# Weights, tokens, keys and vectors handed over in the order of use, and results stored turned, in a GLA, Fourier and PEER inference step

## The chip, the cores and the metric

The kernel runs on one core of one Trainium2 chip. The metric is the device time of one execution in microseconds. The median of the runs of the kernel before is 5125.47 us (3 runs, 5105.1 to 5128.31).

## What is computed

One step of a two-layer network over 128 context tokens and 512 latent tokens of width 1024. Both token groups go through the same layers with the same weights. Cut to what matters (the Fourier part and the rotary embedding are left out):

```python
def _trunk(x, cond, rope_pos, init_state, ...):
    for l in range(DEPTH):                                    # 2 layers
        sh1, sc1, g1, sh2, sc2, g2 = _modulation(cond, w_mod[l], b_mod[l])
        h = _rmsnorm(x, norm1[l]) * (1 + sc1) + sh1
        mix, s_f, s_b = _token_mixer(h, ...)                  # w_in, gated linear attention, Fourier, gates, w_out
        x = x + g1 * mix
        h = _rmsnorm(x, norm2[l]) * (1 + sc2) + sh2
        x = x + g2 * _peer(h, w_query[l], sub_keys[l], expert_u[l], expert_v[l])
    return _rmsnorm(x, final_norm)

def _peer(h, w_query, sub_keys, expert_u, expert_v):
    qry = (x @ w_query).reshape(n, 8, 2, 128)                 # 8 heads, two halves
    s = jnp.einsum('nhpd,hpkd->nhpk', qry, sub_keys)          # 128 keys per half
    ...                                                       # 16 best of each half, 16 best of their sums
    a = jax.nn.gelu(jnp.einsum('nd,nhkd->nhk', xb, expert_u[ib]))
    return jnp.einsum('nhk,nhkd->nd', wb * a, expert_v[ib])   # 128 rows of u and of v for each token
```

## The kernel before, in words

All data are float32. Tokens stand turned in the on-chip memory: `xT` and `hT` hold 128 of the 1024 features on the partitions, 8 chunks, and 640 token columns (128 of the context, then 512 latent). The program is written engine by engine, with semaphores; on each engine the steps of several programs are merged by `weave`, which sorts them by due times in a table, so the order on each engine is fixed when the kernel is built. It runs in stages: the context's mixer of layer 0 with the modulation (0 to 330 us of the trace); the latent mixer of layer 0 with the context's expert stage (to 1051 us); the latent expert stage of layer 0 with the context's mixer of layer 1 (to 2735 us); latent mixer and context experts of layer 1 (to 3488 us); latent experts of layer 1 (to 5053 us); the last norm.

**Weights.** SP (the queue of the sync engine) loads 0.25, 0.5 or 1 MB pieces into four slots of 8 KB a partition, in the order of the list `FILLS`. A piece is loaded as soon as the operand four places before it in the list has been used up (`released`). `cols_of` cuts a piece from the weight matrix in its own layout: 128 partitions, 8 chunks of rows, and runs of 128 or 256 columns, 512 or 1024 bytes. A piece is a `wraw`, `fraw` or `slot` buffer in the rows. In front of the list SP loads the constants and the tokens (`xin`, lines 543 to 546).

**Start.** GpSimd loads fifteen small vectors as rows. TensorE turns vectors and tokens by products with the identity (lines 1093 to 1103), VectorE copies them into `cols` and `xT`, ScalarE and VectorE make `scond`, the gate of the conditioning vectors. Then the modulation begins: 24 products of a layer with 1 MB of `w_mod` each, eight of them ahead of the first norm.

**Keys.** For each of the 8 heads of an expert stage GpSimd loads the two sets of 128 keys (`skey`, two buffers), TensorE turns them (`keys`, line 936), ScalarE copies them (`skT`), and `scores` multiplies the queries with them, one head later. GpSimd loads the key of head h when that of head h-2 has been turned. The expert gathers stand behind the keys in GpSimd's queue.

**Latent merge.** For each z of 8, TensorE makes four products of three terms each (gate of the attention, gate of the Fourier part, both outputs). Each of the four weight pieces is loaded, copied by ScalarE to a rounded high part (`whigh`, `fhigh`) and subtracted by VectorE to a low part (`wlow`, `flow`, line 1576); ScalarE makes the sigmoids and VectorE the gating (`sg`, `mT`) in between. The four pieces of the next z take the four slots as they are used up.

**Expert rows.** For each pick GpSimd gathers 128 rows of 4 KB of `expert_u` and, eight picks later, of `expert_v` (lines 629 and 636), for the latent tokens through rings of six and four buffers. VectorE makes the dot products (line 1731); for the latent tokens TensorE sums the v rows through diagonal matrices, for the context VectorE does (`acc`).

**End.** The last norm writes `hT` (lines 1443 and 1448); TensorE turns it back (line 1088), VectorE copies it to `y_nat` (line 1816), SP stores it in five pieces (lines 594 and 597).

Of the kernel before, what the change touches and what calls it, by code (L numbers as in the profile page):

```python
# [22 lines left out]
F32 = mybir.dt.float32  # L23
# [6 lines left out]
P = 128  # L30
D = 1024
KC = D // P
# [81 lines left out]
def fill_values():  # L114

    loads, values = SLOTS * [0], []
    for n, what in enumerate(FILLS):
        loads[n % SLOTS] += 2 if what[0] == "qk" else 1
        values.append(16 * loads[n % SLOTS])
    return values  # L120
# [106 lines left out]
def build(nc, x_prompt, x_sample, state_gla, c, c_ctx, w_mod, b_mod, norm1, w_in, w_af, b_af, w_ab, b_ab,  # L227
          gla_norm, w_gla_out, w_four_out, w_out, norm2, w_query, sub_keys, expert_u, expert_v, final_norm,
          consts, fourier, y_prompt, y_sample, new_state):
# [26 lines left out]
    cols0 = place("cols0", [P, 24])  # L256
    scond = place("scond", [P, KC, 2])
    cols = [place(f"cols{l}", [P, 80]) for l in range(DEPTH)]
# [72 lines left out]
    def peer_area(s, at, queries_at):  # L331
# [20 lines left out]
        a.skey = [place(f"skey{i}_{tag}", [P, 2, P], at=q) for i in range(2)]  # L352
# [21 lines left out]
    y_nat = [place("y_nat_ctx", [P, NT[CTX], D], at=[zone]), place("y_nat_lat", [P, NT[LAT], D], at=[area[CTX].end])]  # L374
    s_at = [area[LAT].end]
    xin = place("xin", [P, T // P, D], at=s_at)
    rows0 = place("rows0", [24, P], at=s_at)
    rows = [place(f"rows{l}", [80, P], at=s_at) for l in range(DEPTH)]

# [8 lines left out]
    with ExitStack() as ctx:  # L388
# [22 lines left out]
        def sem(name):  # L411
# [3 lines left out]
        s_const, s_tab, s_x, s_rows = sem("const_loaded"), sem("tables_loaded"), sem("x_loaded"), sem("rows_loaded")  # L415
# [7 lines left out]
        s_set, s_xt, s_xc = sem("constants_set"), sem("x_turned"), sem("x_copied")  # L423
        s_rowsT, s_cols = sem("rows_turned"), sem("cols_ready")
# [26 lines left out]
        s_qm, s_qc, s_kt, s_ktc, s_sm, s_sc = (sem("query_mm"), sem("query_copied"), sem("keys_turned"),  # L451
                                              sem("keys_copied"), sem("score_mm"), sem("scores_copied"))
# [8 lines left out]
        s_yt, s_yc = sem("y_turned"), [sem(f"y_copied_of{s}") for s in range(2)]  # L461
# [76 lines left out]
        def cols_of(w, l, c0, width):  # L538
            return w[l][:, c0:c0 + width].rearrange("(c p) n -> p c n", p=P)
# [1331 lines left out]
```

## Time and profile before

| what | value |
|---|---|
| runs, median (lowest to highest) | 5125.47 us (5105.1 to 5128.31) |
| profiled execution, its own time | 5096.34 us |
| its span, first to last instruction | 5094.5 us |
| busy: TensorE, VectorE, ScalarE, GpSimd | 79%, 58%, 26%, 56% of the span |
| moved | 1583.47 MB, 311 GB/s mean |
| of it gathers (queue q0) | 1346.63 MB in 370656 packets, 69.5% of 16 engines |
| of it SP's loads (queue q1) | 229.86 MB in 323856 packets, 14.4% of 16 engines |
| mean granted TensorE clock | 0.952 |

How to read it: a busy share is a mean over stages with different limits; what a stage waits for is read in that stage. In the rows PE is TensorE, PEld its weight loads, DVE VectorE, ACT ScalarE, POOL GpSimd, SPq the queue of SP. A row of the timeline has its start, its length, the engine, the line, what is written and read, how many instructions are merged in it, and in brackets how long the engine stood idle before it and what ended that. A row of DMA issues has the tile, the issuing queue, the count, the size of one and the median time from issue to landing.

### The profile page before, as it was taken

How to read it: one execution, taken by the hardware profiler on the slowest of the kernel's cores; microseconds unless marked ns; L12 is line 12 of the kernel's file. 1: busy time of each engine (PE TensorE's matmuls, PEld its weight loads, DVE VectorE, ACT ScalarE, POOL GpSimd, SP SyncE). 2: the span in 40 equal slices, each digit the busy share in tenths (PEclk: the TensorE clock that was granted, in tenths of full speed). 3: DMA queues.
4: the chain of work that ended last, by engine and by line, in shares of the span. 5: the costliest groups of instructions: out<-in, count | busy, mean ns of one | idle time of the engine just before them, and what ended most of it. 6: DMA issues, size and time to landing. Idle time of an engine off the chain costs nothing. (4 is left out here: it accounts for less than half of the span.)

```text
span 5094.5 us, 43662 instructions
## 1 busy us (share of the span) xinstructions
PE 4028.3 (79%) x13059; PEld 2047.3 (40%) x13059; DVE 2945.2 (58%) x6592; ACT 1314.6 (26%) x2679; POOL 2843.7 (56%) x2611
## 2 busy tenths in 40 slices
PE   7889678898788888788777977889877777776776
PEld 4675346653333333244324543565322222222222
DVE  1127997716555565565543699772556555655644
ACT  2433234511122232233111332451211111111111
POOL 0001665305767776777773066540477777777774
PEclk9999789899999999999999988899999999999999
DMA  6663988737999999999996298882599999999997
GB/s 227 199 186 126 327 321 286 241 95 277 381 397 376 400 396 371 366 400 406 407 390 226 84 337 305 304 268 86 200 366 367 370 393 381 375 382 365 369 392 288
DMA packets 699356, 1583.47 MB, mean 311 GB/s; under 512 B 52344, under 2 KB 368752, under 8 KB 698736
## 3 DMA queue, kind: packets, MB, share of 16 engines
q0 software_dynamic: 370656, 1346.63, 69.5%
q1 hardware_dynamic: 323856, 229.86, 14.4%
q10 hardware_dynamic: 4608, 4.20, 0.2%
q8 instruction: 104, 1.70, 0.1%
q14 instruction: 132, 1.08, 0.1%
HBM read 1575.78 MB, written 4.72 MB: 310 GB/s over the span
## 5 line engine op out<-in xcount | busy, mean ns | idle before, releaser
L657 PE MATMUL pair<-vbuf_lat,diag 128*128 128x512 f32 x4096 | 2024.7, 623 | 705.0 <-DMA vbuf_lat<-in_expert_v,idx_lat 679.3
L657 PEld LDWEIGHTS pair<-vbuf_lat,diag 128*128 128x128 f32 x4096 | 716.1, 192 | 1952.2 <-DMA vbuf_lat<-in_expert_v,idx_lat 1092.8
L636 POOL DMA_INDIRECT vbuf_lat<-in_expert_v,idx_lat x1024 | 1160.2, 1133 | 404.0 <-issue 203.8
L1731 DVE CUSTOM_DVE_ANT_0 ubuf_lat<-hT,ubuf_lat 128x1024 f32<-128x1024 f32 x768 | 935.2, 1224 | 722.9 <-DMA ubuf_lat<-in_expert_u,idx_lat 720.5
L629 POOL DMA_INDIRECT ubuf_lat<-in_expert_u,idx_lat x1024 | 1071.4, 1046 | 418.5 <-issue 234.4
L629 POOL DMA_INDIRECT ubuf_ctx<-in_expert_u,idx_ctx x256 | 289.1, 1129 | 564.7 <-DVE araw L1731 289.9
L1120 ACT ACTIVATE diag<-cst,coef 128x128 f32<-128x128 f32 x1024 | 326.8, 389 | 1064.5 <-DVE coef L1737 1060.6
L657 PE MATMUL pair<-hT,slot 128*128 128x512 f32 (+1 forms) x2048 | 580.7, 444 | 15.0 <-DVE hT L1450 14.9
L1731 DVE CUSTOM_DVE_ANT_0 ubuf_lat<-xnat,ubuf_lat 128x1024 f32<-128x1024 f32 x256 | 311.7, 1224 | 257.8 <-DMA ubuf_lat<-in_expert_u,idx_lat 256.8
L657 PEld LDWEIGHTS pair<-hT,slot 128*128 128x128 f32 x2048 | 322.5, 199 | 257.4 <-issue 254.6
L1120 ACT ACT_TABLE_LOAD x313 | 401.6, 1283 | 77.6 <-DVE mT_lat L1617 50.4
L636 POOL DMA_INDIRECT vbuf_ctx<-in_expert_v,idx_ctx x256 | 291.8, 1140 | 128.2 <-issue 77.7
L1777 DVE SCALAR_TENSOR_TENSOR acc<-vbuf_ctx,coef,acc 128x1024 f32<-128x1024 f32 x254 | 326.3, 1285 | 23.6 <-issue 0.9
L1120 ACT ACTIVATE gel<-araw 128x4 f32<-128x4 f32 x320 | 65.3, 204 | 1029.3 <-DVE araw L1731 1028.7
L1731 DVE CUSTOM_DVE_ANT_0 ubuf_ctx<-hT,ubuf_ctx 128x1024 f32<-128x1024 f32 x256 | 311.7, 1220 | 9.8 <-DMA ubuf_ctx<-in_expert_u,idx_ctx 4.2
L616 POOL DMA_DIRECT2D skey_ctx<-in_sub_keys x16 | 11.5, 720 | 382.3 <-PE pair L936 349.7
L616 POOL DMA_DIRECT2D skey_lat<-in_sub_keys x16 | 11.6, 723 | 314.2 <-PE pair L936 175.5
L657 PE MATMUL pair<-slot,scond 128*2 128x256 f32 x768 | 174.6, 381 | 2.0 <-DVE scond L1837 1.7
L657 PE MATMUL pair<-hmH,whigh 128*128 128x512 f32 x256 | 114.5, 447 | 56.8 <-DVE wlow L1576 45.3
L1649 DVE MAX8 top_lat<-sc_lat 128x8 f32<-128x128 f32 x256 | 55.3, 280 | 166.7 <-ACT sc_lat L1120 163.9
L657 PE MATMUL pair<-slot,hT 128*128 128x256 f32 x640 | 142.2, 381 | 0.0
L657 PE MATMUL pair<-hT,wraw 128*128 128x128 f32 (+1 forms) x768 | 134.6, 330 | 2.4 <-DMA wraw<-in_w_in 1.3
(319 smaller groups left out, 4024.8 us busy)
## 6 DMA issues: line engine op xcount, KB each, us to landing
slot<-in_w_mod SPq DMA_DIRECT2D x48, 1024.0 KB, 7.7
wraw<-in_w_in SPq DMA_DIRECT2D x80, 512.0 KB, 5.2
slot<-in_w_in SPq DMA_DIRECT2D x32, 1024.0 KB, 7.0
slot<-in_w_query SPq DMA_DIRECT2D x32, 1024.0 KB, 5.3
slot<-in_w_in SPq DMA_DIRECT2D x32, 512.0 KB, 4.9
wraw<-in_w_gla_out SPq DMA_DIRECT2D x32, 512.0 KB, 8.6
wraw<-in_w_out SPq DMA_DIRECT2D x32, 512.0 KB, 5.0
ubuf_lat<-in_expert_u,idx_lat POOLq DMA_INDIRECT x1024, 6.5
```

The source lines that it names most:

```text
L616: pool.dma_start(peer[s].skey[h % 2][:, :, :], sub_keys[l, h].rearrange("s k d -> k s d")).then_inc(s_skey[h % 2], 16)
L629: pool.indirect_dma_start(peer[s].u[n % ring_u][:, :], None, u_rows, bass.IndirectOffsetOnAxis(ap=index[:, p // PICKS, p % PICKS:p % PICKS ...
L636: pool.indirect_dma_start(peer[s].v[n % ring_v][:, :], None, v_rows, bass.IndirectOffsetOnAxis(ap=index[:, p // PICKS, p % PICKS:p % PICKS ...
L657: return pe.matmul(out, lhsT, rhs, start=first, stop=last)
L1120: return nc.scalar.activation(out, in_, fn, **kw)
L1649: v.max(a.top[:, h, q, r8], sc[:, h, q, :])
L1731: v.tensor_tensor_reduce(rows_of, x, rows_of, 1.0, 0.0, ALU.mult, ALU.add, araw[n % 3][:, p % GS:p % GS + 1]).then_inc(s_dot, 1)
L1777: last = stt(acc[:, :], row, coef[n % 3][:, j:j + 1], acc[:, :], ALU.mult, ALU.add)
```

## The change

The host hands every input over in the order in which the program takes it (`laid_out`): each weight piece as 128 partitions with one contiguous run of 2, 4 or 8 KB; the columns of query and key of a head as one piece; tokens turned, keys turned, and all small vectors as one array of columns. So the start has no turning and no copies, the keys go straight into `skT`, and the weights come with the same number of loads (one instead of two for query and key) from the same list. SP's first loads are the vectors, the context's tokens and the identity; the rest of the constants goes ahead of fill 8, the latent tokens ahead of fill 16. GpSimd loads the key of head h when the scores of head h-2 are made. The result is stored from `hT` as it stands, the latent part in four pieces as the norm goes, and the host turns it back.

```diff
+def laid_out(inputs):
...
+    def chunks(w, width):
+
+        l, rows, columns = w.shape
+        return w.reshape(l, rows // P, P, columns // width, width).transpose(0, 3, 2, 1, 4)
+
+    def turned(x):
+        return x.reshape(-1, KC, P).transpose(2, 1, 0)
...
+    out["w_mod"] = chunks(f["w_mod"], WCOLS)
+    out["w_qk"] = np.concatenate([chunks(w_in[:, :, c0:c0 + QK_W], P) for c0 in (Q0, K0)], 4)
...
+    out["sub_keys"] = f["sub_keys"].transpose(0, 1, 4, 2, 3)
...
         def _(sp):
+            sp.dma_start(columns[:, :], vectors).then_inc(s_cols, 16)
+            sp.dma_start(xT[:, :, COLS[CTX]], x_prompt).then_inc(s_x, 16)
             sp.dma_start(cst[:, 0:C_ROT], consts[:, 0:C_ROT]).then_inc(s_const, 16)
-            sp.dma_start(xin[:, 0, :], x_prompt[0]).then_inc(s_x, 16)
-            sp.dma_start(xin[:, 1:T // P, :], x_sample[0].rearrange("(t p) d -> p t d", p=P)).then_inc(s_x, 16)
-            sp.dma_start(cst[:, C_ROT:C_W], consts[:, C_ROT:C_W]).then_inc(s_tab, 16)
             for f, what in enumerate(FILLS):
+                if f == MOD_FIRST:
+                    sp.dma_start(cst[:, C_ROT:C_W], consts[:, C_ROT:C_W]).then_inc(s_tab, 16)
+                if f == 2 * MOD_FIRST:
+                    sp.dma_start(xT[:, :, COLS[LAT]], x_sample).then_inc(s_x, 16)
...
                 if kind == "mod":
-                    sp.dma_start(full[:, :, :], cols_of(w_mod, l, what[2] * WCOLS, WCOLS)).then_inc(s_slot[w], 16)
+                    sp.dma_start(full[:, :, :], w_mod[l, what[2]]).then_inc(s_slot[w], 16)
...
-                    sp.dma_start(dst[:, :, :], cols_of(src, l, c0 + z * P, P)).then_inc(s_slot[w], 16)
+                    sp.dma_start(dst[:, :, :], (w_zg, w_zf, w_gla_out, w_four_out)[i][l, z]).then_inc(s_slot[w], 16)
...
+            hold(sp, s_h[CTX], (2 * DEPTH + 1) * KC)
+            sp.dma_start(y_prompt, hT[:, :, COLS[CTX]]).then_inc(s_y, 16)
+            for k in range(0, KC, 2):
+                hold(sp, s_h[LAT], 2 * DEPTH * KC + k + 2)
+                sp.dma_start(y_sample[:, k:k + 2, :], hT[:, k:k + 2, COLS[LAT]]).then_inc(s_y, 16)
...
             def load_keys(l, s):
                 for h in range(PH):
                     n = (2 * l + s) * PH + h
-                    hold(pool, s_kt, n - 1)
-                    pool.dma_start(peer[s].skey[h % 2][:, :, :], sub_keys[l, h].rearrange("s k d -> k s d")).then_inc(s_skey[h % 2], 16)
+                    hold(pool, s_sm, 2 * (n - 1))
+                    pool.dma_start(peer[s].skT[h % 2][:, :, :], sub_keys[l, h]).then_inc(s_skey[h % 2], 16)
...
-            def keys(l, s, h, dst):
+            def keys_loaded(l, s, h):
                 pe.wait_ge(s_skey[h % 2], 16 * ((2 * l + s) * (PH // 2) + h // 2 + 1))
-                for j in range(2):
-                    last = pe.transpose(dst[:, j * P:(j + 1) * P], peer[s].skey[h % 2][:, j, :], ident)
-                last.then_inc(s_kt, 1)
...
                 def scores(h):
                     pe.wait_ge(s_qc, 2 * (n0 + h + 1))
-                    pe.wait_ge(s_ktc, n0 + h + 1)
+                    keys_loaded(l, s, h)
...
             pe.wait_ge(s_const, 16)
-            pe.wait_ge(s_rows, 48 + 96 * DEPTH)
-            pe.transpose(ps[7][:, 0:24], rows0[:, :], ident[0:24, 0:24]).then_inc(s_rowsT, 1)
...
+            pe.wait_ge(s_set, 1)
             pe.wait_ge(s_cond, 1)
```

Where instructions stand. SP's queue at the start of the program, before (`xin` is the tokens' buffer, `cst` the constants, `slot` a weight slot, `wlr` and `wab` small operands of the decay gates):

```order
L543 DMA cst<-table_consts 128x256
L544 DMA xin<-in_x_prompt 128x1024
L545 DMA xin<-in_x_sample 128x4x1024
L546 DMA cst<-table_consts 128x2176
L553 DMA slot_76<-in_w_mod 128x8x256
```

and after, with the places of the fills 8 and 16 (four `w_mod` pieces and the middle of the list left out by "..."):

```order
L569 DMA columns<-in_vectors 128x184
L570 DMA xT<-in_x_prompt 128x8x128
L571 DMA cst<-in_consts 128x256
L582 DMA slot_74<-in_w_mod 128x2048
...
L582 DMA slot_95<-in_w_mod 128x2048
L574 DMA cst<-in_consts 128x2176
L592 DMA wlr_ctx<-in_w_lr 128x256
...
L582 DMA slot_95<-in_w_mod 128x2048
L576 DMA xT<-in_x_sample 128x8x512
L596 DMA wab<-in_w_af 16x128
L597 DMA wab<-in_w_ab 16x128
L598 DMA slot_74<-in_w_qk 128x2048
```

The first weight piece moves up from the fifth to the fourth place, the two large loads move behind the eighth and the sixteenth piece, and a piece is one run of 2048 elements instead of eight of 256.

TensorE's queue in the context's expert stage of layer 0, before (`slot` holds the query weights, `ones` sums the squares of a norm):

```order
L657 MATMUL pair<-hT,ones 128x128 x8
L936 MATMUL pair<-cst,skey_ctx 128x128 x2
L657 MATMUL pair<-hT,slot_76 128x128 x16
L936 MATMUL pair<-cst,skey_ctx 128x128 x2
L657 MATMUL pair<-hT,slot_83 128x128 x16
L657 MATMUL pair<-skT_ctx,qry_ctx 128x128 x2
L936 MATMUL pair<-cst,skey_ctx 128x128 x2
L657 MATMUL pair<-hT,slot_90 128x128 x16
```

and after:

```order
L673 MATMUL pair<-hT,ones 128x128 x8
L673 MATMUL pair<-hT,slot_74 128x128 x16
L673 MATMUL pair<-hT,slot_81 128x128 x16
L673 MATMUL pair<-skT_ctx,qry_ctx 128x128 x2
L673 MATMUL pair<-hT,slot_88 128x128 x16
```

The key turnings are gone, 32 pairs in the program, with 32 copies on ScalarE; nothing else changes place on TensorE, VectorE or ScalarE there.

TensorE's queue at the end, before:

```order
L657 MATMUL pair<-vbuf_lat,diag_234 128x512 x8
L657 MATMUL pair<-vbuf_lat,diag_235 128x512 x8
L948 MATMUL pair<-cst,out_nat_220 128x128 x8
L657 MATMUL pair<-hT,ones 128x512 x8
L1088 MATMUL pair<-cst,hT 128x128 x32
```

and after:

```order
L673 MATMUL pair<-vbuf_lat,diag_228 128x512 x8
L673 MATMUL pair<-vbuf_lat,diag_229 128x512 x8
L962 MATMUL pair<-cst,out_nat_214 128x128 x8
L673 MATMUL pair<-hT,ones 128x512 x8
L420 UNCONDITIONAL_BRANCH
```

The 32 turnings behind the last norm are gone, and with them four copies on VectorE; the stores wait for the norm itself.

## Rows read from the trace of the kernel before

**Rows 1.** Windows: stretch, length; PE, PEld, DVE, ACT, POOL busy; clock, DMA, GB/s

```profile
330.00:1051.00 721.00, 589.68 (x2195) 386.85 (x2194) 555.17 (x919) 263.05 (x349) 291.40 (x257) 0.88 0.70 243
1200.00:2735.00 1535.00, 1231.71 (x3672) 539.19 (x3672) 853.99 (x2185) 369.81 (x925) 1116.23 (x1014) 0.98 1.01 386
3640.00:5053.00 1413.00, 1017.85 (x2076) 356.29 (x2076) 816.55 (x2023) 215.68 (x671) 1088.12 (x1012) 0.99 0.99 376
```

**Rows 2.** Timeline of TensorE at the start: first instruction and first modulation product

```profile
14.25 0.27 PE L1093 MATMUL pair<-cst,rows 24*128 24x24 f32 x1 [14.25 <-DMA rows<-in_b_ab]
...
24.83 3.61 PE L657 MATMUL pair<-slot,scond 128*2 128x256 f32 x16 [1.72 <-DVE scond L1837]
```

**Rows 3.** Windows of the first loads (as rows 1), and the first load's issue row

```profile
2.00:4.00 2.00, 0.00 (x0) 0.00 (x0) 0.00 (x0) 0.00 (x0) 2.00 (x5) 1.00 0.95 256
4.00:6.00 2.00, 0.00 (x0) 0.00 (x0) 0.00 (x0) 0.00 (x0) 2.00 (x5) 1.00 1.00 361
...
cst<-table_consts SPq DMA_DIRECT2D x1, 128.0 KB, 2.1
```

**Rows 4.** Groups by form on TensorE, 17 to 20 and 1192 to 1196 us

```profile
L1103 PE MATMUL pair<-cst,xin 128*128 128x128 f32 x16 | 3.6, 403 | 0.0
...
L942 PE MATMUL pair<-cst,hT 128*128 128x128 f32 x24 | 3.0, 275 | 0.2 <-ACT hT L1120 0.2
```

**Rows 5.** DMA issues: 60 to 300 (two), 1500 to 2000, 2000 to 2500, 3235 to 3450

```profile
slot<-in_w_mod SPq DMA_DIRECT2D x14, 1024.0 KB, 5.1
wraw<-in_w_in SPq DMA_DIRECT2D x20, 512.0 KB, 4.6
...
slot<-in_w_mod SPq DMA_DIRECT2D x11, 1024.0 KB, 15.9
...
wraw<-in_w_in SPq DMA_DIRECT2D x15, 512.0 KB, 18.5
...
fraw<-in_w_four_out SPq DMA_DIRECT2D x7, 256.0 KB, 9.2
```

**Rows 6.** Latent merge: sum of fourteen windows; VectorE's waits, 3235 to 3409; its timeline

```profile
sum 342.42, PE 297.08 PEld 236.43 DVE 282.84 ACT 176.12 POOL 172.58; mean PE 21.22 PEld 16.89 DVE 20.20 ACT 12.58 POOL 12.33
...
DVE wlow L1576 <- ACT whigh L1120: 23.3, 10, 5.8
...
DVE flow L1576 <- ACT fhigh L1120: 3.7, 1, 3.7
...
3265.15 1.23 DVE L1576 TENSOR_TENSOR wlow<-wraw,whigh 128x1024 fp32r<-128x1024 f32 x1 [5.85 <-ACT whigh L1120]
...
3308.12 1.23 DVE L1576 TENSOR_TENSOR wlow<-wraw,whigh 128x1024 fp32r<-128x1024 f32 x1 [4.17 <-ACT whigh L1120]
```

**Rows 7.** Timeline: key turnings on TensorE, latent and context, and ScalarE's key copy

```profile
3516.81 0.38 PE L936 MATMUL pair<-cst,skey_lat 128*128 128x128 f32 x2
3517.03 13.90 PE L657 MATMUL pair<-hT,slot 128*128 128x512 f32 x32
...
2739.30 0.66 PE L936 MATMUL pair<-cst,skey_ctx 128*128 128x128 f32 x2 [4.62 <-DMA skey_ctx<-in_sub_keys]
...
312.68 0.38 ACT L1120 ACTIVATE skT_ctx<-pair 128x256 f32<-128x256 f32 x1
```

**Rows 8.** DMA queues: packets, MB, share; 1420 to 2620 (two), 3640 to 5040

```profile
q0 software_dynamic: 114374, 416.47, 88.2%
q1 hardware_dynamic: 74240, 50.52, 13.0%
...
q0 software_dynamic: 144445, 525.98, 98.8%
```

**Rows 9.** Timeline of the end: last norm, turning, stores

```profile
5082.31 1.67 DVE L1448 TENSOR_SCALAR hT<-hT,cols 128x512 f32<-128x512 f32 x4
5084.03 6.08 PE L1088 MATMUL pair<-cst,hT 128*128 128x128 f32 x32 [11.20 <-DVE hT L1448]
...
5087.35 4.53 SPq L597 DMA_DIRECT2D out<-y_nat_lat  x4
```

More of the change, by code:

```diff
@@ L117, in fill_values @@
     for n, what in enumerate(FILLS):
-        loads[n % SLOTS] += 2 if what[0] == "qk" else 1
+        loads[n % SLOTS] += 1
         values.append(16 * loads[n % SLOTS])
@@ L224, with build @@
     pass
-def build(nc, x_prompt, x_sample, state_gla, c, c_ctx, w_mod, b_mod, norm1, w_in, w_af, b_af, w_ab, b_ab,
-          gla_norm, w_gla_out, w_four_out, w_out, norm2, w_query, sub_keys, expert_u, expert_v, final_norm,
-          consts, fourier, y_prompt, y_sample, new_state):
+VECTORS = (("b_mod", 48), ("norm1", 8), ("norm2", 8), ("gla_norm", 8), ("b_af", 4), ("b_ab", 4))
+def laid_out(inputs):
+    f = {name: np.asarray(a) for name, a in inputs.items()}
+    def chunks(w, width):
[3 more added lines that the diff above has]
+        return x.reshape(-1, KC, P).transpose(2, 1, 0)
+    w_in = f["w_in"]
+    out = {"x_prompt": turned(f["x_prompt"]), "x_sample": turned(f["x_sample"])}
+    head = [f["c"], f["c_ctx"], f["final_norm"]]
+    layers = [f[name][l] for l in range(DEPTH) for name, _ in VECTORS]
+    out["vectors"] = np.concatenate([a.reshape(-1, P).T for a in head + layers], 1)
+    out["w_mod"] = chunks(f["w_mod"], WCOLS)
+    out["w_qk"] = np.concatenate([chunks(w_in[:, :, c0:c0 + QK_W], P) for c0 in (Q0, K0)], 4)
+    out["w_v"] = chunks(w_in[:, :, V0:V0 + V_W], DV)
+    out["w_r"] = chunks(w_in[:, :, R0:R0 + V_W], DV)
+    out["w_lr"] = chunks(w_in[:, :, L0:L0 + 2 * LOWRANK], 2 * LOWRANK)
+    out["w_u"] = chunks(w_in[:, :, U0:U0 + F_W], P)
+    out["w_zg"] = chunks(w_in[:, :, ZG0:ZG0 + D], P)
+    out["w_zf"] = chunks(w_in[:, :, ZF0:ZF0 + D], P)
+    out["w_gla_out"] = chunks(f["w_gla_out"], P)
+    out["w_four_out"] = chunks(f["w_four_out"], P)
+    out["w_out"] = chunks(f["w_out"], P)
+    out["w_query"] = chunks(f["w_query"], WCOLS)
+    out["sub_keys"] = f["sub_keys"].transpose(0, 1, 4, 2, 3)
+    for name in ("w_af", "w_ab", "state_gla", "expert_u", "expert_v"):
+        out[name] = f[name]
+    out["consts"], out["fourier"] = constants()
+    return {name: np.ascontiguousarray(a) for name, a in out.items()}
+def build(nc, x_prompt, x_sample, vectors, w_mod, w_qk, w_v, w_r, w_lr, w_u, w_zg, w_zf, w_gla_out, w_four_out, w_out,
+          w_query, sub_keys, w_af, w_ab, state_gla, expert_u, expert_v, consts, fourier, y_prompt, y_sample, new_state):
     u_rows = expert_u.rearrange("l e d -> (l e) d")
@@ L1812, in last_norm @@
                 norm(s, 2 * DEPTH, lambda k: cols0[:, 16 + k:17 + k], lambda k: None)
-                for t in range(NT[s]):
-                    yield at(34.0 + 10.0 * t)
-                    dve.wait_ge(s_yt, s * NT[0] + t + 1)
-                    v.tensor_copy(y_nat[s][:, t, :], pair[3 - t % 2][:, :]).then_inc(s_yc[s], 1)
             v.memset(ones[:, :], 1.0)
```

135 lines of the change are left out of this document (31 added, 104 removed).

## The prediction, made before the changed kernel had run

> **What bounds the kernel now.** I read the stretches by busy time first [rows 1]. The latent tokens' expert stage fills two of them, 1200 to 2735 us and 3640 to 5053 us: there the 16 DMA engines are busy 1.01 and 0.99 of the time at 386 and 376 GB/s, while no compute engine is above 0.80. These stages last as long as their expert rows take to arrive. In the first of them the mixer of the context's second layer is woven in, so weights share the DMA engines with the gathers; in the second nothing is loaded but expert rows. The rest belongs to the compute engines: the first 330 us (context mixer, modulation) to TensorE's queue, 330 to 1051 us (latent mixer, context experts) to VectorE and TensorE together (555 and 590 of 721 us), and their twin of layer 1, 2735 to 3488 us, likewise. So a cheaper load pays only where a load ends a wait, and an instruction taken away pays only where its engine is the late one. I go through the stages in that order.
>
> **Start.** Before, TensorE begins at 14.25 us, when the last of fifteen small vector loads is in, turns vectors and tokens for ten microseconds, and runs the first modulation product at 24.83 us [rows 2]. After, that product waits for `scond` and the first 1 MB of `w_mod`. `scond` needs the vector load (a first load lands in 2.1 us after its issue at 1.1 us [rows 3]), two exponentials and four short VectorE steps: about 6 us. Ahead of the first `w_mod` megabyte stand 0.09 MB of vectors, 0.52 MB of tokens, 0.13 MB of constants and two keys of 0.13 MB: 2.06 MB with itself. At 256 GB/s from 2 to 4 us and 361 GB/s after that [rows 3] the last byte moves at 8.3 us; with under a microsecond to the semaphore the product starts at 9.0 us, 15.8 us earlier. Against it stands TensorE's speed: the turning matmuls between 17 and 20 us took 403 ns each, the same kind later 275 ns [rows 4]. The engine had been idle until 14 us and ran at its lower level, 1.2 GHz by these durations (the clock column says 1.00 there, so I go by the durations). Today the turning bears that slow stretch, some 5 us long; after the change the first two products do, and half of it, 2.5 us, is given back. Net **-13.3 us**; bounds -11 and -16. The later positions of the 1.09 MB of constants and the 2 MB of latent tokens (SP's queue, ahead of fills 8 and 16) delay the fills behind them by 3 and 6 us at these rates; a fill is asked for four operands ahead of its use and lands in 5.1 us [rows 5], and four operands hold TensorE for over 13 us in this stage, so I cost them at nothing. If that cover failed, each delay would count once.
>
> **Keys.** A pair of key transposes takes 0.22 us of TensorE (3516.81 to 3517.03) and, for the context, the copy of the turned keys (0.38 us [rows 7]) holds ScalarE between the query copy and the score copy for which TensorE waits; part of it runs beside the score product, so I count 0.2 us of it. Seven heads of each pass count, the first is hidden behind the wait for the norm: context 7 x 0.42 = 2.9 us in each layer, latent 7 x 0.22 = 1.5 us in each. In layer 1 the context's first query also waits 4.62 us for its key, which the gather queue may load only when the last latent update is done [rows 7]. After, keys are wanted only by the scores, two products later; the query starts right behind that update; I count 3.5 of the 4.62, since the update's last steps lie in them. GpSimd now waits for the scores of head h-2 and no longer for a transpose: that is one product later, still a whole query product ahead of the use, and the gathers behind it on GpSimd wait for chosen experts long after. Sum: 2 x 2.9 + 2 x 1.5 + 3.5 = **-12.3 us**; bounds -8 and -15.
>
> **Weights while the gathers run.** With no gather beside it, a 1 MB load in runs of 1 KB lands in 5.1 us and a 0.5 MB load in runs of 512 B in 4.6 us; under full gathering they take 15.9 and 18.5 us [rows 5]. Both are 1024 packets, 64 for each DMA engine. So what they pay for is the number of turns against the gathers' 4 KB packets. After, 1 MB and 0.5 MB are 128 packets, 8 for each engine: 8 turns of a gather packet (0.988 x 1400 x 16 / 144445 = 0.153 us each [rows 8]) and a weight packet of the same size give 2.5 us and, with a first load's 2.1 us, some 4.5 us.
> Where does that pay? In the latent merge (the loop over `z`, 84 matmuls a turn). Elsewhere the loads are asked for early enough that next to no engine waits for one; the context's merge of layer 0 does for a few microseconds in all, which I leave out. The fourteen turns from the first to the last start of a `z` in both layers take 342.4 us, 24.5 us each, with VectorE busy 20.2 us and TensorE 21.2 us of one [rows 6]. VectorE goes through its queue in order and stands for the high parts that ScalarE copies from the loaded weights: 23.3 and 3.7 us in the seven turns of layer 1 [rows 6], 3.9 us a turn. Behind it on VectorE stand the expert dots and the gating, for which ScalarE waits in turn. Two causes are in it. For the second to fourth part the load is late, as at 3265.15 us (5.85 us; `w_four_out`, 256 KB, takes 9.2 us to land here [rows 5]). For the first part it is ScalarE, which comes to it at the end of its sigmoids, as at 3308.12 us (4.17 us). The first kind goes, the second stays and takes back some of it. I count the half, a little less: 1.7 us a turn, 22.8 us instead of 24.5, 14 x 1.7 = **-24 us**. Bounds: 0, if ScalarE's chain holds the turn where it is, and 14 x 3.2 = -45, where TensorE is never idle.
> The first gather stage is told by bytes. In 1420 to 2620 us, 416 MB of rows and 50.5 MB of weights came in; gathers alone at the other stage's rate (525.98 MB in 1400 us, 376 GB/s) would have been 451 MB [rows 8]. So a megabyte of weights displaced 0.69 MB of rows. Larger packets can cut either way. If a megabyte then displaces a whole one, 15.8 MB more are late: +42 us. If weights occupy the engines at the gathers' rate (416 MB in 0.882 x 1200 us, 394 GB/s, against 50.5 MB in 0.130 x 1200 us, 324 GB/s), they free 28 us: -28. I take **0**, since the total moved does not change and the engines are full either way; both ends stay.
>
> **End.** VectorE is done with the last norm at 5083.98 us; then 32 transposes and four copies lead to four stores, the last issued by 5091.88, and the span ends 2.6 us later at 5094.5 [rows 9]. After, the last store is issued as the norm ends: 5083.98 + 0.4 + 2.6 = 5087.0, and half a microsecond more since two stores of 0.5 MB come 0.85 us apart: **-7 us**; bounds -6 and -8.
>
> **Sum.** -13.3 - 12.3 - 24 + 0 - 7 = -56.6 us on the profiled execution's 5096.34 us (span 5094.5 and 1.84 around it): 5039.7. The median of the runs is 5125.47, 1.0057 times that; so **5069 us**.
>
> **Rivals.** *The merge keeps its pace.* For it: the second kind of wait, which no load ends; against it: the first kind, on VectorE, of which 20.2 us a turn are busy. Then -32.6 us, 5093. The Trainium skill (DMA: Bandwidth & Descriptors, Specifications) puts the smallest transfer for line rate at 512 B. By that rule every weight run already moves at full rate, the loads would land as late as now, and the time would be this rival's; the rows with equal landings for equal packet counts speak against it, since no bandwidth rule gives 0.5 MB the time of 1 MB.
> *Weights push the rows back byte for byte*: +42, so -14.6 us, 5111. For it: the engines are full; against it: today's 0.69.
> *Fewer packets free the engines*: -28 more, 5040.
> *Slower.* One mechanism: in the first gather stage an 8 KB packet holds an engine for two gather packets, rows land later than the rings of six and four buffers cover, and the gather queue runs empty behind each fill. The saving is used up from 1.11 MB displaced for each MB of weights ((34.7 + 56.6 x 0.376) / 50.5), half a percent is lost from 1.30; at 2 MB it is +176 us, 5245. Against it: today's 15.9 us landings come in bursts too, without that.
> *The layout doesn't arrive as runs*: the order of both kernels shows one run of 2048 elements a partition, so I give it nothing of its own.
>
> **How the numbers follow.** Forecast 0.50, merge unchanged 0.20, byte for byte 0.12, freed engines 0.13, slower 0.05. A measurement of this kernel tells some 0.5% (26 us) from no change. Below 5099.8 lie nearly all of the forecast (0.48), of the merge rival two thirds (0.13), of byte for byte a third (0.04) and the freed engines (0.13): 0.78. Within 0.5%: 0.17. Slower: 0.05. The range takes in the merge rival, the byte rival and most of the freed engines: 5030 to 5112.
>
> **What would show it.** The first modulation product near 9 us with doubled matmul times; no idle before the context's first query in layer 1 beyond the update; weight loads landing in 4 to 6 us in 1500 to 2500 us where they took 16; VectorE's wait for the second to fourth high parts gone and the fourteen turns near 318 us; the first gather stage unchanged within 10 us, with 390 GB/s or so in all; the end 3 us behind the last norm. Wrong it is above all if the merge's turns stay at 24 us, or if the gathers' megabytes in that stage fall while weights land faster.

## The result, and the profile of the changed kernel

The changed kernel takes 5076.23 us (median of 16 runs) where the kernel before takes 5104.72 (16 runs): ratio 0.9938, 95% interval 0.9922 to 0.9953, some 32 us faster. The forecast was 5069 us and a gain of 57. Its profiled execution took 5081.04 us with a span of 5079.1, only 15.3 us below the profiled execution of before; the stages below are read from these two, and the experiments show how much of that small distance is chance.

First the three stretches of [rows 1] in the changed kernel (windows; columns as there):

```profile
330.00:1051.00 721.00, 592.31 (x2180) 383.50 (x2179) 562.36 (x933) 263.13 (x345) 293.00 (x260) 0.89 0.67 242
1200.00:2735.00 1535.00, 1221.13 (x3624) 544.19 (x3624) 833.60 (x2115) 364.09 (x909) 1080.29 (x995) 0.97 0.99 380
3640.00:5053.00 1413.00, 1017.64 (x2076) 355.80 (x2076) 809.01 (x1997) 215.21 (x667) 1079.75 (x1005) 0.99 0.99 375
```

The second gather stage is what it was (375 GB/s against 376). The first one moves 380 GB/s where it moved 386, and its DMA share is 0.99 where it was 1.01: the stage in which the weights share the DMA engines with the expert rows got worse. Its two ends, the first latent gather on GpSimd and the last of the sixteen latent updates on VectorE, stand in the timelines; first the kernel before, then the changed one:

```profile
1177.57 1.01 POOL L629 DMA_INDIRECT ubuf_lat<-in_expert_u,idx_lat  x1 [32.35 <-DVE wts_lat L1722]
2734.72 1.12 DVE L1747 SCALAR_TENSOR_TENSOR xT<-pair,modT,xT 128x128 f32<-128x128 f32 x4 [0.81 <-PE pair L948]
```

```profile
1149.87 0.99 POOL L647 DMA_INDIRECT ubuf_lat<-in_expert_u,idx_lat  x1 [1.26 <-DVE wts_lat L1704]
2742.57 1.13 DVE L1729 SCALAR_TENSOR_TENSOR xT<-pair,modT,xT 128x128 f32<-128x128 f32 x4 [0.81 <-PE pair L962]
```

The stage begins 27.7 us earlier and ends 7.9 us later: 1558.3 us became 1593.8 (from the start of the gather to the end of the update). Everything won before it, and more, is handed back in it. Cut at events that both kernels have (the products with `ones` that sum a norm's squares, and those two rows), the two profiled executions differ so: up to the first context expert norm -14.9 us, from there to the latent norm -0.7, latent mixer and context experts of layer 0 -10.8, latent queries -1.2, **first gather stage +35.6**, context queries of layer 1 -4.4, latent mixer of layer 1 -12.9, latent queries -1.2, second gather stage +0.5, end -5.2. The sum is -15.4 but for rounding.

What the DMA engines moved in 2 to 4 us (windows), then TensorE's timeline at the start and at the context's first query of layer 1:

```profile
2.00:4.00 2.00, 0.00 (x0) 0.00 (x0) 0.00 (x0) 0.86 (x1) 0.91 (x2) 1.00 0.67 117
```

```profile
10.61 5.22 PE L673 MATMUL pair<-slot,scond 128*2 128x256 f32 x16 [10.61 <-DMA slot<-in_w_mod]
...
16.50 3.61 PE L673 MATMUL pair<-slot,scond 128*2 128x256 f32 x16
...
2743.75 9.04 PE L673 MATMUL pair<-hT,slot 128*128 128x128 f32 x64 [1.22 <-DVE xT L1729]
```

The modulation begins with its own weights at 10.61 us instead of 24.83 [rows 2]; one product is slow (5.22 us), the second takes its 3.6 us. The query of layer 1 follows the update by 0.05 us, where the key was waited for 4.62 us [rows 7].

The DMA issues of 1500 to 2000 us and, last row, of 2000 to 2500 us (last column: median us to landing):

```profile
slot<-in_w_mod SPq DMA_DIRECT2D x10, 1024.0 KB, 7.8
...
wab<-in_w_af SPq DMA_DIRECT2D x2, 8.0 KB, 3.6
...
wraw<-in_w_zf SPq DMA_DIRECT2D x8, 512.0 KB, 6.6
```

The sum of the fourteen merge windows, and VectorE's waits in the merge of layer 1 (us in total, times, longest):

```profile
sum 321.76, PE 289.81 PEld 231.51 DVE 282.77 ACT 177.44 POOL 176.54; mean PE 20.70 PEld 16.54 DVE 20.20 ACT 12.67 POOL 12.61
```

```profile
DVE wlow L1558 <- ACT whigh L1104: 14.4, 9, 2.5
...
DVE flow L1558 <- ACT fhigh L1104: 0.8, 2, 0.5
```

Weights land in 7.8 and 6.6 us where they took 15.9 and 18.5 [rows 5], and the merge's fourteen turns take 321.8 us where they took 342.4 [rows 6]. The end, VectorE's timeline and the windows of TensorE's sum of squares ahead of it:

```profile
5073.68 1.67 DVE L1429 TENSOR_SCALAR hT<-hT,columns 128x512 f32<-128x512 f32 x4
```

```profile
5055.00:5058.00 3.00, 2.99 (x7) 1.54 (x8) 1.13 (x4) 3.00 (x7) 0.00 (x0) 0.56 0.00 0
...
5059.00:5064.00 5.00, 5.00 (x13) 1.98 (x11) 0.00 (x0) 0.69 (x1) 0.00 (x0) 1.00 0.00 0
```

The last norm is done at 5075.35 us and the span ends 3.75 us later, where it was 10.5 [rows 9].

The totals of all queues in 1420 to 2620 us, before and after; the DMA queues of the changed kernel in the same stretch (packets, MB, share of the 16 engines' time), beside [rows 8]; and what GpSimd waits for in 1200 to 2700 us, before (L636) and after (L654):

```profile
DMA packets 189825, 468.72 MB, mean 391 GB/s; under 512 B 14149, under 2 KB 88101, under 8 KB 189766
```

```profile
DMA packets 123814, 458.63 MB, mean 382 GB/s; under 512 B 13829, under 2 KB 15077, under 8 KB 120428
```

```profile
q0 software_dynamic: 112188, 408.50, 88.6%
q1 hardware_dynamic: 10416, 48.42, 10.1%
```

```profile
POOL vbuf_lat L636 <- PE pair L657: 84.5, 141, 4.8
```

```profile
POOL vbuf_lat L654 <- PE pair L673: 133.2, 138, 5.1
```

This is the reading that the prediction lacked. The weights' share of the engines fell from 13.0 to 10.1%, as the rival of the freed engines had it. But the gathers did not take the time that came free: their share stood still (88.2, now 88.6%) and their bytes fell from 416.47 to 408.50 MB. So each of their packets takes longer: by the prediction's way of reckoning (share x 1200 x 16 / packets) 0.1481 us before and 0.1516 us now, 2.4% more. GpSimd, which issues the gathers, stands 133 us instead of 85 for buffers of the second table's rows that TensorE hasn't yet read; whether that wait is a cause of the later rows or comes of them, these lines don't tell.

### The profile page after: what moved, and what is told of

Read it like the earlier page. It is cut to its first block and busy times, and to the rows that moved or that the text cites. A ratio compares the mean times of both kernels' runs of the same rounds, so it can differ in the third digit from the quotient of the medians.

```text
span 5079.1 us, 43269 instructions
## 1 busy us (share of the span) xinstructions
PE 4012.7 (79%) x12912; PEld 2037.2 (40%) x12912; DVE 2933.3 (58%) x6574; ACT 1306.9 (26%) x2647; POOL 2819.7 (56%) x2596
## 3 DMA queue, kind: packets, MB, share of 16 engines
q1 hardware_dynamic: 50592, 229.95, 12.3%
## 5 line engine op out<-in xcount | busy, mean ns | idle before, releaser
L654 POOL DMA_INDIRECT vbuf_lat<-in_expert_v,idx_lat x1024 | 1155.1, 1128 | 454.0 <-PE pair L673 229.4
L654 POOL DMA_INDIRECT vbuf_ctx<-in_expert_v,idx_ctx x256 | 296.3, 1157 | 126.6 <-issue 77.4
L673 PE MATMUL pair<-slot,scond 128*2 128x256 f32 x768 | 176.3, 383 | 10.9 <-DMA slot<-in_w_mod 10.6
```

Source lines behind the costliest of these rows:

```text
L654: pool.indirect_dma_start(peer[s].v[n % ring_v][:, :], None, v_rows, bass.IndirectOffsetOnAxis(ap=index[:, p // PICKS, p % PICKS:p % PICKS ...
L673: return pe.matmul(out, lhsT, rhs, start=first, stop=last)
```

## The experiments

In the table, "first" and "second" are the lengths of the two gather stages, read as above from each kernel's own profile; the ratio is to the kernel before, with its 95% interval.

| kernel | weights while the first stage runs | first, us | second, us | ratio |
|---|---|---|---|---|
| before | cut by columns, runs of 1 KB and 512 B | 1558 | 1452 | 1 |
| changed | one run of 8 or 4 KB a partition | 1594 | 1453 | 0.9938 [0.9922, 0.9953] |
| again | the same | 1594 | 1446 | 0.9937 [0.9916, 0.9957] |
| cut_first_gather | cut by columns in this stage alone | 1569 | 1437 | 0.9873 [0.9856, 0.9891] |
| cut_all | cut by columns everywhere | 1559 | 1441 | 0.9929 [0.9910, 0.9948] |
| runs_only | as changed; start, keys and end as before | 1608 | 1445 | 1.0002 [0.9988, 1.0016] |
| pieces_8_runs | dense, 8 runs of 1 KB / 512 B | 1567 | 1466 | 0.9900 [0.9868, 0.9931] |
| pieces_2_runs | dense, 2 runs of 4 / 2 KB | 1578 | 1445 | 0.9934 [0.9914, 0.9953] |
| pieces_16_runs | dense, 16 runs asked for, not all given | 1608 | 1453 | 0.9955 [0.9932, 0.9977] |
| paced_quarters | 8 KB runs, four quarters in turn | 1792 | 1438 | 1.0357 [1.0303, 1.0411] |
| extra_long | as changed; 46 pieces more later | 1594 | 1542 | 1.0123 [1.0080, 1.0166] |
| extra_cut | as changed; the same 46, cut | 1585 | 1504 | 1.0046 [1.0024, 1.0069] |
| rings_5_5_long | as changed, rings of 5 and 5 | 1582 | 1440 | 0.9878 [0.9839, 0.9917] |
| rings_5_5_cut | as cut_first_gather, rings of 5 and 5 | 1560 | 1434 | 0.9860 [0.9815, 0.9905] |

The second stage loads no weights except in the two extra kernels; without these it lies between 1434 and 1466 us. So two single executions can lie some 30 us apart by chance, and a length is read below only where several kernels or the ratio, which comes from 4 to 16 runs, bear it out.

**Which part makes the stage longer?** Four kernels: the changed one again, two that take the weights' layout back in one stage or in all, and one that has the layout alone. In their expectations theory 1 blames the long runs, theory 2 chance, theory 3 another part of the change.

again (no edit):

> The changed kernel once more, as the control for its first gather stage. In the first profile of it the stage (first latent gather to the last of the sixteen latent updates, before: 1177.6 to 2735.8 us, 1558 us) lasted 1149.9 to 2743.7 us, 1594 us: 36 us more, where the prediction had 0 with a bound of +42. Theory 1 (large weight runs cost the gathers time): the stage lasts 1580 to 1605 us again, the ratio to before is 0.993 to 0.995. Theory 2 (the stage varies by that much from one execution to the next, whatever the layout): 1550 to 1600, and any of the four kernels of this group may show either end.

cut_first_gather:

```diff
+def cut(kind, l, s):
+    return l == 1 and s == CTX and kind != "query"
...
-                    sp.dma_start(full[:, :, :], w_mod[l, what[2]]).then_inc(s_slot[w], 16)
+                    sp.dma_start(full[:, :, :], cols_of(w_mod_rows, l, what[2] * WCOLS, WCOLS) if cut("mod", l, CTX) else w_mod[l, what[2]]).then_inc(s_slot[w], 16)
...
```

> The changed kernel, but the weights that are loaded while the first gather stage runs (layer 1's modulation and the mixer of its context: 50 MB) are read as before, cut out by columns in runs of 1 KB and 512 B; all else as changed. Theory 1 (the large runs of this stage cost the gathers 20 to 36 us): the stage is back at 1555 to 1570 us and the kernel is faster than the changed one by 20 to 35 us, ratio to before 0.987 to 0.990. Theory 2 (scatter): no difference from the changed kernel beyond 0.2%, 0.993 to 0.995. Theory 3 (the stage is longer for another part of the change, such as the queries that start earlier or the start): 0.993 to 0.995 too, with the stage at 1580 to 1600 us.

cut_all (the same edit with `return True`):

> The changed kernel with all weight pieces read as before, cut out by columns; start, keys, tokens and end stay changed. Theory 1: the first gather stage is back at 1555 to 1570 us; the start keeps its 13 to 15 us, queries and keys some 10, the end 5; the latent merge loses its gain (the seven turns at 170 to 172 us where the changed kernel has 161): ratio 0.992 to 0.995, that is slower than the version with only the first gather stage's weights cut by 20 to 25 us. Theory 2: 0.992 to 0.995 likewise, but the stage anywhere in 1550 to 1600. Theory 3: the stage at 1580 to 1600 us, ratio 0.998 to 1.001.

runs_only (an edit of the kernel before):

```diff
-                    sp.dma_start(full[:, :, :], cols_of(w_mod, l, what[2] * WCOLS, WCOLS)).then_inc(s_slot[w], 16)
+                    sp.dma_start(full[:, :, :], w_mod1[l, what[2]]).then_inc(s_slot[w], 16)
...
```

> The kernel before with only the weight pieces handed over as contiguous runs; start, keys, tokens and end as before. Theory 1: the merges gain 9 to 12 us in each layer, the first gather stage loses 20 to 36: ratio 0.999 to 1.003. Theory 2: 0.994 to 0.997, since only the merge's gain is left. Theory 3: 0.995, with the stage at 1555 to 1570 us.

All four ratios, and the stage's lengths where theory 1 named them, came out as it said; the other two fall. Two of its guesses missed: in runs_only the stage loses 50 us in its profile, not 20 to 36, and cut_all's merge of layer 1 takes 174.0 us, not 170 to 172. With long runs the stage lasts 1594, 1594 and 1608 us (and 1594 and 1585 in the two extra kernels below, which are the changed kernel up to there), with cut ones 1558, 1569 and 1559, whatever the rest of the kernel is. cut_first_gather differs from the changed kernel by the layout in this stage only and is 33 us faster (0.9937 to 0.9873 of some 5110). The layout by itself, in runs_only, is worth nothing: what it wins in the merges it loses here. Start, keys and end alone, in cut_all, are worth 0.7%. The queues of cut_first_gather in 1420 to 2620 us, and its landing in 1500 to 2000 us:

```profile
q0 software_dynamic: 114269, 416.09, 88.5%
q1 hardware_dynamic: 67907, 48.08, 12.3%
```

```profile
slot<-in_w_mod_rows SPq DMA_DIRECT2D x10, 1024.0 KB, 14.3
```

The same 48 MB of weights in 6.5 times the packets, and 7.6 MB more of expert rows in the same time. A packet of the gathers' queue takes 0.1487 us, reckoned as above. This number scatters far less than the lengths do: in this stretch it is 0.1481 to 0.1487 us in every kernel with cut columns or eight runs, and 0.1510 to 0.1526 in every kernel with one long run or two (0.1497 with sixteen; paced_quarters, below, stands apart).

**Is it the length of the runs, the burst, or the place in memory?** A piece is one 1 MB or 0.5 MB load. Four kernels keep the pieces dense in memory and change how they arrive in this stage. Theory A blames the length of a packet, theory B the short burst in which a piece arrives, theory C the place in memory.

pieces_8_runs (and the same with `RUNS = 2` and 16):

```diff
+RUNS = 8
...
+        out[name + "_pieces"] = a.reshape(len(a), P, RUNS, -1).transpose(0, 2, 1, 3)
...
+                to = dst[:, :, :].rearrange("p c n -> p (c n)").rearrange("p (r n) -> p r n", r=RUNS)
+                nc.sync.dma_start(to, pieces[z].rearrange("r p n -> p r n")).then_inc(semaphore, 16)
```

> The changed kernel, but each weight piece loaded during the first gather stage is handed over dense in memory as eight blocks, so that it arrives in eight runs a partition (1 KB, or 512 B for the half pieces), the packet count of the old layout without its columns cut from far rows. First gather stage so far: 1594 us with one run, 1559 to 1569 with the old column cuts. Theory A (a long packet costs the row queues their turn) and theory B (a megabyte in one short burst does): 1555 to 1572 us, total as with the cut columns, ratio 0.986 to 0.990. Theory C (the memory serves the column cuts' scattered addresses better than dense blocks): 1585 to 1600 us, ratio 0.993 to 0.995.

> As the one with eight runs, but two runs a partition (4 KB and 2 KB): the packet is as long as an expert row's at most, the piece lands in an estimated 9 to 10 us. Theory A (length of a packet, twice a row's is the harm): most of the loss is gone, 1565 to 1580 us. Theory B (the loss goes with the time the piece is spread over): about a quarter of it gone, 1580 to 1592 us. Theory C: 1585 to 1600.

> As the one with eight runs, but sixteen runs a partition (512 B and 256 B), 2048 packets a piece, landing in an estimated 25 to 32 us. Theory B: the spread is wider still, 1545 to 1562 us, unless a piece now lands after TensorE wants it. Theory A: no further gain over eight runs, 1555 to 1572 us. Theory C: 1585 to 1600. If the number of packets itself costs the engines time, it is longer than with eight runs: above 1575 us.

paced_quarters:

```diff
+            step = P // PARTS
+            for i in range(PARTS):
+                if i:
+                    hold(nc.sync, s_slot[w], FILL_VALUE[f] - 16 * (PARTS - i))
+                nc.sync.dma_start(dst[i * step:(i + 1) * step, :, :], source[i * step:(i + 1) * step]).then_inc(s_slot[w], 16)
```

> The changed kernel with its long runs (8 and 4 KB), but during the first gather stage each piece is asked for in four quarters of 32 partitions, each when the one before has landed, so that a piece is spread over some 12 to 16 us with the packets as long as they are. Theory B (the burst): the stage falls to 1558 to 1575 us, ratio 0.986 to 0.990. Theory A (the length of a packet): 1585 to 1600 us, ratio 0.993 to 0.995. Theory C: 1585 to 1600.

Landing of a modulation piece in 1500 to 2000 us with eight runs and with two:

```profile
slot<-in_w_mod_pieces SPq DMA_DIRECT2D x10, 1024.0 KB, 13.7
```

```profile
slot<-in_w_mod_pieces SPq DMA_DIRECT2D x10, 1024.0 KB, 9.1
```

Theory C, that scattered addresses are served better, is out: dense pieces of eight runs give 1567 us and 0.9900, like the cut ones; the interval of the ratio just reaches 0.993. Two runs win nothing clear: one execution has 1578 us, but the ratio, 0.9934, is that of the changed kernel, and a row packet takes 0.1510 us as with long runs:

```profile
q0 software_dynamic: 112924, 411.19, 88.8%
```

So most of the loss is still there when a weight packet is no longer than an expert row's 4 KB, against theory A as it was put; the quarter of the loss that theory B expected to go is too small to be seen. Sixteen runs are not what they were meant to be for the megabyte pieces: these land in 10.9 us where 25 to 32 were expected, and of packets from 512 B to just under 2 KB there are only 832 (14638 less 13806), where one piece would have 2048 (1500 to 2000 us, the totals and a landing):

```profile
DMA packets 64666, 189.16 MB, mean 378 GB/s; under 512 B 13806, under 2 KB 14638, under 8 KB 64641
...
slot<-in_w_mod_pieces SPq DMA_DIRECT2D x11, 0.5 KB, 10.9
```

Only the smaller pieces came in the short runs asked for, 256 B and less. Beside them (2000 to 2500 us) just 169.17 MB of rows came with 16.22 MB of weights, and the weights take 15.1% of the engines:

```profile
q0 software_dynamic: 46459, 169.17, 86.2%
q1 hardware_dynamic: 71723, 16.22, 15.1%
...
wraw<-in_w_gla_out_pieces SPq DMA_DIRECT2D x8, 512.0 KB, 20.0
```

With eight runs it is 177.10 MB beside 18.08 in the same stretch, for 12.5%. So shorter is not always better, and a long landing alone (20.0 us here) doesn't do the good either. Whether short packets or long landings do the good was for paced_quarters to tell, and it told little: a quarter took 6.1 us, so that a piece took 24 and not 12 to 16, and the rows themselves landed in 9.1 us instead of 6.5 (1500 to 2000 us):

```profile
slot<-in_w_mod SPq DMA_DIRECT2D x40, 256.0 KB, 6.1
...
vbuf_lat<-in_expert_v,idx_lat POOLq DMA_INDIRECT x146, 9.1
```

Pieces that come too late (TensorE stands 104 us for weights in 1200 to 2700 us, and not at all in the changed kernel) and rows that are slower for a reason that I can't read there are both in its 1792 us. It shows only that long runs spread out in this way are far from a cure.

**What does a piece cost where no mixer is woven in?** In the second gather stage TensorE has nothing but the expert rows. There two kernels load 46 unused pieces, one every ten expert places. Theory R says that long runs cost by way of TensorE: a late row holds up its queue with the mixer work in it, and the row buffers come free late.

extra_long, and extra_cut with `cols_of(w_mod_rows, 1, i % MODS * WCOLS, WCOLS)` as its source:

```diff
+            for i in range(46):
+                f = len(FILLS) + i
+                w = f % SLOTS
...
+                hold(sp, s_pv[LAT], NT[LAT] * PICKS + 40 + 10 * i)
+                sp.dma_start(slot[w][:, :, :], w_mod[1, i % MODS]).then_inc(s_slot[w], 16)
```

> The changed kernel with 46 megabyte pieces more (48.2 MB, never used) loaded in the second gather stage, one every ten expert places, in runs of 8 KB. There no mixer work stands in TensorE's queue, so this measures the price of a piece for the gathers by itself. That stage lasts 1437 to 1466 us in the profiles so far. Byte for byte at its 376 GB/s the pieces cost 128 us. Theory R (long runs cost because a late row holds up TensorE's queue with its mixer work, and the row buffers come free late): the price is the same here in long runs and in cut ones, 110 to 130 us each. Theory A (a long packet by itself takes more from the rows): 20 us or more dearer than the cut form.

> The same 46 extra pieces in the second gather stage, cut out by columns in runs of 1 KB as the kernel before loads them. Theory R: 110 to 130 us, within 10 us of the long form. Theory A: 20 us or more cheaper than the long form. If two queues at work get more out of the engines wherever they meet (0.69 MB of rows displaced for one of weights, as in the first stage before), 80 to 95 us.

The same pieces cost 95 us long (1.0123 - 0.9937 of 5110) and 56 us cut: 39 us apart for 48.2 MB, without any mixer work. Theory R in its strict form, the same price for both, is refuted; theory A has the sign and the size. Neither costs its bytes (128 us), and the cut form costs less even than the 80 to 95 us of the last guess. The totals of 3700 to 5000 us tell how: first the changed kernel without extra pieces, then extra_long and extra_cut, each with the landing of its pieces.

```profile
DMA packets 135306, 489.79 MB, mean 377 GB/s; under 512 B 14927, under 2 KB 15951, under 8 KB 135255
```

```profile
DMA packets 132925, 503.11 MB, mean 387 GB/s; under 512 B 14667, under 2 KB 15691, under 8 KB 127500
...
slot<-in_w_mod SPq DMA_DIRECT2D x43, 1024.0 KB, 8.1
```

```profile
DMA packets 175709, 516.74 MB, mean 397 GB/s; under 512 B 15034, under 2 KB 61008, under 8 KB 175660
...
slot<-in_w_mod_rows SPq DMA_DIRECT2D x44, 1024.0 KB, 15.9
```

With a second queue at work the engines move more than the gathers alone get from them in this stretch: 13.3 MB more with long runs, 27.0 MB more with cut ones. Long pieces are under way for 43 x 8.1 = 348 us of the 1300, cut ones for 44 x 15.9 = 700. Both come to some 38 GB/s above the gathers' rate for as long as a piece is under way. That is worked out from two kernels and doesn't carry over: by the same sum the first stage of the changed kernel gives some 14 GB/s (458.63 MB against 376 x 1.2 = 451.2, pieces under way for some 540 us). No run holds the packet length and changes the time alone, so it is not shown to be the cause. GpSimd's waits for second-table buffers in the same stretch, without extra pieces, with long and with cut ones:

```profile
POOL vbuf_lat L654 <- PE pair L673: 68.4, 211, 1.8
```

```profile
POOL vbuf_lat L679 <- PE pair L698: 119.5, 170, 4.2
```

```profile
POOL vbuf_lat L679 <- PE pair L698: 40.3, 74, 2.7
```

Long pieces lengthen this wait as they do in the first stage, and cut ones don't.

**Are the buffers the way by which it costs?**

rings_5_5_long and rings_5_5_cut (the latter on cut_first_gather):

```diff
-U_RING, V_RING = (4, 6), (4, 4)
+U_RING, V_RING = (4, 5), (4, 5)
```

> The changed kernel with the latent rows' buffers shared out as five for the first table and five for the second, where it has six and four (no memory is left for more). GpSimd waits 121 to 133 us for second-table buffers in the first gather stage with long runs, 83 to 107 with cut ones. Theory R: with a fifth buffer the wait falls by a third or more and the stage from 1594 to 1560 to 1580 us, unless the first table's five run out in their place. Theory A: no change beyond 10 us.

> The version with cut columns in the first gather stage and the rings of five and five. Theory R: less is to be had here, the stage from 1569 to 1555 to 1566 us and the ratio 0.984 to 0.988, so the fifth buffer narrows the distance between long and cut runs from 25 us to under 15. Theory A: 25 us between the two as with six and four.

GpSimd's waits in 1200 to 2700 us with long runs:

```profile
POOL ubuf_lat L647 <- DVE araw L1713: 97.0, 23, 12.7
POOL vbuf_lat L654 <- PE pair L673: 49.5, 89, 5.1
```

The wait for second-table buffers falls to 49.5 us from 121 to 133, and 97 us for the first table's five come up in its place (18 to 21 with six). By the ratio the fifth buffer wins 31 us with long runs (0.9938 to 0.9878) and 7 with cut ones (0.9873 to 0.9860, within the intervals). The distance between the two forms, 33 us with six and four, is now 9 us by the ratios, 19 by the medians (5053.1 and 5033.8 us of four runs each) and 22 by the stages (1582 and 1560 us). Theory R wanted it under 15 and theory A at 25, and these numbers don't decide between them. In the engines nothing has moved closer (1420 to 2620 us, long, then cut):

```profile
DMA packets 122596, 454.19 MB, mean 378 GB/s; under 512 B 13694, under 2 KB 14942, under 8 KB 119210
...
q0 software_dynamic: 111114, 404.59, 87.5%
```

```profile
DMA packets 182189, 462.72 MB, mean 386 GB/s; under 512 B 13993, under 2 KB 80777, under 8 KB 181618
...
q0 software_dynamic: 113442, 413.10, 87.8%
```

A row packet takes 0.1512 and 0.1486 us, as before. So the division of the buffers is worth something by itself; how much of the price of long runs goes by way of the buffers stays open. rings_5_5_cut, at 0.9860, is the fastest kernel measured, though its interval holds cut_first_gather's 0.9873; both beat the changed kernel.

## Why the prediction was right, and where it was not

The time (5069 forecast, 5076.2 measured, range 5030 to 5112) and the sign were right, but that the time came within 7 us is luck. The gain was half of what was forecast: 28 us between the medians, 32 by the ratio, 15 in the pair of profiles, for 57. The forecast started from 5125.47 us, the median of three runs, and the kernel's median of sixteen is 20.8 us lower; from that the same gain would have led to 5048. The mechanism was right for the start, the keys, the merge and the end, whose terms were a little too large or small, and wrong for one term:

- **Start**, -13.3 forecast: -14.2 at the first product, -14.9 when the mixer is through. The product came at 10.61 and not at 9.0 us. The load was slower than taken (117 GB/s moved in 2 to 4 us where 256 was assumed), which by the windows up to 9 us makes 2.06 MB late by some 0.6 us; the other microsecond lies behind those bytes, where 0.7 us was assumed up to the product and it was 1.7. In return one product was slow and not two. The later loads of constants and latent tokens cost nothing that the stage shows.
- **Keys**, -12.3 forecast. From the update to the last context score it is -2.8 us in layer 0 and -6.8 in layer 1 (forecast 2.9, and 2.9 + 3.5), the latent queries give -1.2 each (forecast 1.5): -12.0. Not all of it reaches the path at once, since the latent mixer runs beside the context's scores: 7.6 us appear in these stages, and part of the 3.0 us that the mixer stages win beyond their merges may be the rest.
- **Merge**, -24 forecast: 342.4 - 321.8 = -20.7 us (9.0 and 11.7 in the two layers). The reason held. VectorE's waits for the high parts fell from 27.0 to 15.2 us in layer 1: those for the second to fourth part from 15.7 to 5.3, those for the first, which I had put down to ScalarE's own work, only from 11.2 to 9.9. The longest is 2.5 us where it was 5.85. cut_all, with the old loads, has 171.8 and 174.0 us for seven turns, so the gain is the weights'. The landing was mis-sized, 6.6 and 7.8 us instead of 4.5: I put 2.1 us under it as a load's own time, from the idle start, but beside the gathers even an 8 KB load takes 3.6 us.
- **First gather stage**, 0 forecast, the step that failed. "I take 0, since the total moved does not change and the engines are full either way": the total did change, from 391 to 382 GB/s, in the engines that looked full. Measured are +35.6 us in the pair of profiles and, by the ratios, some 33 in cut_first_gather against the changed kernel. The bounds of that step held it (-28 and +42), and the rival *byte for byte* has its mechanism nearest: (0.376 x 1200 - 408.5) / 48.42 = 0.88 MB of rows displaced by a megabyte of weights, for the 0.69 of before. It is not quite one for one, and the extra pieces show that the price of a megabyte is no constant but depends on how it comes: 0.44 MB cut and 0.74 MB long in the second stage (56 and 95 us x 0.376 / 48.2).
- **End**, -7 forecast: the piece behind the norm is 6.8 us shorter. 1.6 us of it are lost ahead of the norm, where the sum of squares took 8.65 us instead of 7.03. TensorE's clock was granted at 0.56 in 5055 to 5058 us, mostly its lower level of 1.2 GHz, and at 1.00 from 5059. The engine had stood idle for 1.1 and 1.3 us just before, but so it had in the kernel before, at a clock of 1.00. That the change does it isn't shown: the same sum takes 7.03 us in cut_first_gather and 8.54 in again.

Without the first gather stage the terms come to -14.9 - 7.6 - 23.7 - 5.2 = -51.4 us (start, queries, mixers, end), against -56.6 forecast. The rivals: *the merge keeps its pace* fell with the 321.8 us. *Fewer packets free the engines* is the instructive one, because half of it came true. The packets did free 2.9% of the engines' time, but the rows came no faster for it: their share stayed and each of their packets took 2.4% longer. *Slower* didn't happen, its price of 2 MB a megabyte being far from 0.88.

What I had in hand and didn't use: [rows 8] give the gathers alone 376 GB/s and the two queues of the mixed stage 389 (391 with all queues). Engines that move more when a second queue joins in are not full with the first, however near 1 their share reads: the share counts the time of packets, and a row packet's time differs (0.153 us in the second stage, 0.148 beside the short runs). I used the two numbers to price a megabyte and took the price as a property of the bytes. It was a property of those loads. Why a row packet is quicker beside short runs than beside long ones, no run here shows.

## What to carry to other kernels

Long contiguous runs made a load land sooner (a megabyte in 7.8 us for 15.9), and that pays where an engine waits for that load: here in the merges, 21 us. Beside a saturating stream of gathers nobody waited for the weights, and there the old short runs (512 B to 1 KB) were better by about 30 us: choose the layout stage by stage, by what ends the waits there. When the mixed rate of a stage lies above the rate of its main stream alone, the price of the second stream depends on the form of its loads, and a change of that form has to be priced anew: here eight runs of 1 KB or 512 B were the cheapest form of those tried, one and two long runs were dearer, and so were runs of 256 B.

## What the runs showed of the hardware that I had not expected

- Extra pieces beside the gathers raised the total, and in short runs more than in long ones: 397 GB/s with 1 KB runs, 387 with 8 KB, 377 with no pieces. The Trainium skill (Perfetto Trace Analysis, DMA Optimizations) holds that small DMAs, under 2 KB, carry a significant overhead for each transfer and that larger ones, such as 4 or 8 KB, can improve throughput where DMA is the bound. Read as a rule for runs, these kernels agree with it for the landing of a piece (15.9 us with 1 KB, 8.1 with 8 KB) and disagree for the total beside a gather stream.
- Packets of 256 B and less do cost: in 2000 to 2500 us 71,723 packets, nearly all of this kind, took 15.1% of the engines for 16.22 MB. In eight runs, mostly of 512 B, 18.08 MB took 12.5%, and in one run 17.44 MB took 8.8%.
- A quarter piece of 32 partitions took 6.1 us beside the gathers, hardly less than the whole piece's 7.8, and the rows landed in 9.1 us instead of 6.5. The quarters took more of the engines too: 14.9% for 19.97 MB in 1500 to 2000 us, where whole pieces took 10.4% for 20.74. Why stays open.
